# A two-layer decoder trunk on one core: the second mixer's attention is started four dense steps sooner

## The reference

```
q, k, v, qi, ki, wi = split(h @ w_in)          # h: normed x, 512 x 1024
q, k, qi, ki = rope(q), rope(k), rope(qi), rope(ki)
score = sum over 8 heads of relu(qi . ki) * wi # per query block of 128, causal
idx   = top_k(score, 128)
s     = (q . k) / 8, kept only where the key is in idx and causal
out   = softmax(s) @ v
x     = x + norm(out @ w_out)
```

## Time and profile before

| | us |
|---|---|
| median of 3 runs | 1124.03 |
| lowest and highest run | 1121.41, 1128.97 |
| the profiled execution's own time | 1121.3 |
| its span, first to last instruction | 1119.5 |
| TensorE matmul busy | 1077.3 (96%) |
| VectorE busy | 743.7 (66%) |
| ScalarE busy | 542.5 (48%) |
| GpSimd busy | 192.6 (17%) |

### The profile page before, as it was taken

How to read it: one execution, slowest core, us unless ns; L and a number is a source line. 1 busy time by engine, 2 the same in 40 slices (tenths; PEclk the granted TensorE clock), 3 DMA queues, 4 the chain that set the end, 5 groups by cost and what they waited for, 6 DMA issues and landing times. The chain is left out here.

```text
span 1119.5 us, 14906 instructions
## 1 busy us (share of the span) xinstructions
PE 1077.3 (96%) x5433; PEld 865.6 (77%) x5433; DVE 743.7 (66%) x1284; ACT 542.5 (48%) x1014; POOL 192.6 (17%) x338
## 2 busy tenths in 40 slices
PE   7999999999999999999989978999999999999996
PEld 6766678988888888888667755668988888888885
DVE  4354544577688697687478878644587698696684
ACT  6376653445435444435454466653445444444431
POOL 1344530000000000005312368440000000000004
PEclk9999999999999999999999989999999999999998
DMA  7431403824445455422433314003734455355401
GB/s 229 94 77 38 99 16 73 172 62 102 101 106 111 85 113 113 91 61 49 94 76 76 76 39 113 2 1 83 163 71 102 90 113 113 77 112 113 99 15 76
DMA packets 50793, 97.84 MB, mean 87 GB/s; under 512 B 4448, under 2 KB 4640, under 8 KB 50720
## 3 DMA queue, kind: packets, MB, share of 16 engines
q1 hardware_dynamic: 50208, 96.78, 38.7%
q10 hardware_dynamic: 512, 0.11, 0.0%
HBM read 94.78 MB, written 2.10 MB: 87 GB/s over the span
## 5 line engine op out<-in xcount | busy, mean ns | idle before, releaser
L1920 PE MATMUL bank<-r_hi,w_hi 128*128 128x512 f32 (+1 forms) x456 | 177.5, 389 | 0.0
L1921 PE MATMUL bank<-r_hi,w_lo 128*128 128x512 f32 (+1 forms) x456 | 177.4, 389 | 0.0
L1922 PE MATMUL bank<-r_lo,w_hi 128*128 128x512 f32 (+1 forms) x456 | 177.4, 389 | 0.0
L1536 DVE TENSOR_TENSOR w_lo<-w_raw,w_hi 128x1024 fp32r<-128x1024 f32 x84 | 102.1, 1223 | 70.7 <-ACT w_hi L1082 70.6
L1082 ACT ACTIVATE w_hi<-w_raw 128x1024 fp32r<-128x1024 f32 x84 | 87.7, 1055 | 118.8 <-PE bank L1922 82.9
L2261 PE MATMUL bank<-w_hi,hid_hi 128*128 128x512 f32 x336 | 130.7, 389 | 0.0
L2262 PE MATMUL bank<-w_lo,hid_hi 128*128 128x512 f32 x336 | 130.7, 389 | 0.0
L2263 PE MATMUL bank<-w_hi,hid_lo 128*128 128x512 f32 x336 | 130.7, 389 | 0.0
L1091 ACT ACTIVATE w_hi<-w_raw,gT 128x512 fp32r<-128x512 f32 x96 | 64.6, 716 | 107.6 <-DMA w_raw<-in_w_mlp_up 76.1
L776 POOL TENSOR_TENSOR acc<-acc,G 128x512 f32<-128x512 f32 x8 | 13.0, 1653 | 594.3 <-ACT waste L950 594.3
L1930 PE MATMUL bank<-w_hi,r_hi 128*128 128x512 f32 x240 | 101.4, 423 | 5.2 <-DVE w_lo L1313 3.5
(11 more groups left out here) (198 smaller groups left out, 2135.7 us busy)
## 6 DMA issues: line engine op xcount, KB each, us to landing
w_raw<-in_w_mlp_up SPq DMA_DIRECT2D x64, 512.0 KB, 6.5
w_raw<-in_w_mlp_down SPq DMA_DIRECT2D x64, 512.0 KB, 6.9
w_raw<-in_b_w_in SPq DMA_DIRECT2D x16, 512.0 KB, 6.5
w_raw<-in_a_w_in SPq DMA_DIRECT2D x8, 512.0 KB, 6.5
w_raw<-in_a_w_out SPq DMA_DIRECT2D x8, 512.0 KB, 5.9
w_raw<-in_b_w_out SPq DMA_DIRECT2D x8, 512.0 KB, 6.2
X<-in_x SPq DMA_DIRECT2D x4, 512.0 KB, 6.6
w_raw<-in_a_w_in SPq DMA_DIRECT2D x8, 256.0 KB, 7.3
```

The source lines that it names most:

```text
L1536: nc.vector.tensor_tensor(half_of(w_lo[:, u % 2, :], a), b_of(PRODUCTS[i][1], a), half_of(w_hi[:, u % 2, :], a).bitcast(f32), ALU.subtract ...
L1920: nc.tensor.matmul(bank, whi, xhi, start=start, stop=False)
L1921: nc.tensor.matmul(bank, wlo, xhi, start=False, stop=False)
L1922: return nc.tensor.matmul(bank, whi, xlo, start=False, stop=stop)
```

## The change

Four dense steps of the input projection (16 to 19) move from ahead of the loop into it, so the loop starts after step 15, and with them two query tiles (14, 15). The fill table has 18 steps in place of 14: steps 16 to 23, then output steps 0 to 9 as before but in later iterations. The order of pairs takes both query blocks 0 and 1 of one head half first. The high and low halves of output weights 60 to 63 come in later iterations, as do the transposes of updated X blocks 0 and 1. Block 2 has had 3 top-k rounds when the loop starts, where it had 7, and the schedule of rounds in the loop is new.

```diff
-         ((0, 0), (1, 0), (0, 1), (1, 1), (0, 2), (1, 2), (0, 3), (1, 3)))
+         ((0, 0), (0, 1), (1, 0), (1, 1), (0, 2), (1, 2), (0, 3), (1, 3)))
...
-FILL_IN = (12, 20)
+FILL_IN = (12, 16)
...
-        {0: (0,), 1: (1,), 3: (2,), 4: (3,), 5: (4,), 6: (5,), 7: (6,), 8: (7,), 10: (8,), 11: (9,), 12: (10,), 13: (11,),
-         14: (12,), 15: (13,)})
+        {-1: (0, 1), 0: (2,), 1: (3,), 2: (4,), 3: (5,), 5: (6,), 6: (7,), 8: (8,), 9: (9,), 10: (10, 11), 11: (12,), 12: (13,), 13: (14,), 14: (15, 16), 15: (17,)})
...
-          {-1: ((2, 0),), 0: ((2, 1),), 4: ((2, 2),), 5: ((2, 3),)})
-H_TURN = ({13: (0,), 15: (1,)}, {10: (0,), 15: (1,)})
-
-SPLITS = ({-1: (4,), 1: (5,), 6: (6,), 8: (7,), 9: (8,), 10: (9,)}, {1: (60,), 4: (61,), 5: (62,), 6: (63,)})
+          {-1: ((1, 2),), 0: ((1, 3),), 2: ((2, 0),), 3: ((2, 1),), 7: ((2, 2),), 8: ((2, 3),)})
+H_TURN = ({13: (0,), 15: (1,)}, {13: (0,), 16: (1,)})
+
+SPLITS = ({-1: (4,), 1: (5,), 6: (6,), 8: (7,), 9: (8,), 10: (9,)}, {4: (60,), 6: (61,), 7: (62,), 8: (63,)})
...
-FILL_OUT = (12, 4)
+FILL_OUT = (12, 8)
...
-                    for qn in range(12, 18):
+                    for qn in range(12, 16):
...
             split(59)
-            q_high(1, 14)
-            q_high(1, 15)
-            q_scaled(1, 2, 0)
-            q_scaled(1, 2, 1)
...
             split(59)
-            q_low(1, 14)
-            top_rounds(2, 5)
-            q_low(1, 15)
-            top_rounds(2, 7)
-
-
-            ROUNDS_2 = (8, 9, 10, 12, 13, 14, TOPK // 8)
-            ROUNDS_3 = (0, 1, 2, 3, 4, 5, 6, 8, 10, 12, 14, TOPK // 8)
+
+
+            ROUNDS_2 = (5, 7, 9, 11, 13, 14, TOPK // 8)
+            ROUNDS_3 = (0, 1, 2, 3, 4, 6, 8, 10, 12, 14, 15, TOPK // 8)
...
-            for s in range(8, 20):
+            for s in range(8, 16):
                 in_work(1, s)
...
                 if s in (12, 13):
                     queries_turned(1, s)
-                if s in (16, 17):
-                    queries_turned(1, s - 2)
```

More of the change, by code:

```diff
@@ L195, in t_order @@
         order += [("q", 8), ("q", 9), ("ki_tok",), ("q", 10), ("ki_back",), ("q", 11), ("k", 4), ("k", 5), ("k", 6)]
-        order += [("k", 7), ("q", 12), ("q", 13), ("q", 14), ("q", 15)]
+        order += [("k", 7), ("q", 12), ("q", 13)]
     for n in range(-1, 17):
```

## The result

The changed kernel takes a median of 1128.51 us (20 runs, 1126.20 to 1129.67), the kernel before 1122.12 us beside it (20 runs, 1120.63 to 1128.97). The ratio is 1.0047, interval 1.0037 to 1.0057: by it some 5.3 us slower. That is clear of no change, but less than the 1% that I called telling. The profiled execution's own time is 1126.2 us, where the one before had 1121.3.

A forecast was written before the change was run, and what follows sets the result against it. VectorE was taken to bound the stage up to turn 8's mask, 2.8 us sooner; TensorE's road behind it goes from 87.4 to 94.1, ending the stage 3.8 later: 1121.3 + 3.8 = 1125.1, given as 1126, range 1116 to 1132.

The forecast's parts named there:

- Turn 8 masked: End of turn 8's masked scores, the first turn with three key blocks: at 685.5 us, 2.8 us sooner than before.
- VectorE's waits: Avoidable waits in VectorE's chain up to turn 8's mask: 1.31 + 1.73 + 0.5 + 1.53 = 5.1 us taken out.
- The term of 3.0 us for two more rounds: Block 3 has 11 rounds, not 9, by turn 8's masked scores: 2 x 1.52 = 3.0 us more for VectorE.
- From turn 9's first scores to the end: TensorE's road behind turn 8's mask to the stage's end: 94.1 us, where it was 87.4.
- the wait of query 19's transposes: Behind turn 8's mask, a bank copy waits for ScalarE's high half of an output weight: 1.2 us, between 0 and 1.9.
- the waits of 1.39 and 1.24: Two TensorE waits behind turn 8's mask in the kernel before, said to be lost because three more steps cover them.
- the X block in iteration 16: The second X block's transposes have no step beside them: between 0 and 1.9 us, taken as 0.5.
- The gaps: TensorE's gaps from 626 to 685 add up to more than before, the longest put down to VectorE.
- The steps filling the waits: First rival: four moved steps of 2.84 us fill TensorE's idle time and come out whole, 1110 us; chance 7%.
- Half of them: Second rival: VectorE's small waits are more than taken out, turn 8 masked at 680, about 1119 us; chance 25%.
- GpSimd late: Third rival: unit 63's low half ends after TensorE wants it at 704.8, +4 to +7, so 1129 to 1132; chance 13%.
- (c): Pair order in the loop: turns of one and two key blocks change places, changing nothing in the sum to turn 8's mask.

The follow-up runs named there:

- the thinned steps: Changed kernel with nine of twelve matmuls left out of three dense steps ahead of turn 8's mask (ratio to before 1.0044), or three output steps behind it (1.0009).
- the rounds left out: Changed kernel without the first eight top-k rounds of block 3; ratio to the kernel before 0.9964.
- the reverse edit: Kernel before with the changed kernel's schedule of block 3's rounds, two more ahead of turn 8's last masked scores; ratio to the kernel before 1.0000.
- the two edits: Changed kernel with block 3's old schedule of rounds and output weights' high halves behind the next iteration's first copies; ratio to the kernel before 0.9998.
- The one-step version: Kernel before with only dense step 19 and query tile 14 moved into the loop; ratio to the kernel before 0.9982, median 1120.17 us beside 1122.82.
- (rounds): Changed kernel with the kernel before's schedule of block 3's rounds; ratio to the kernel before 1.0032.
- (high halves): Changed kernel with ScalarE's high halves of output weights behind the next iteration's first copies in layer 1; ratio to the kernel before 1.0028.

## Why the prediction was right

**The bound.** That the changed kernel's stage is VectorE's up to turn 8's mask and in the main TensorE's after it is shown from both sides: by the thinned steps and by the rounds left out.

**Turn 8 masked** was said for 685.5 and came at 684.8; the first scores for "about 626" and came at 626.09. VectorE's waits, which I took out of its chain, are out: ahead of the last masked scores of turn 8 only the reciprocals' 0.9 us waits and small ones are left. From the common start to the mask its busy time rose by 1.8 us (51.71 to 53.52), just the 3.0 for rounds less the 1.2 for what falls later; its idle time fell by 5.3 (13.38 to 8.05), where I had 5.1 less 0.5. That 0.7 is the difference. It comes with one of my own signs of being wrong, reciprocal waits under 0.7 us: three are some 0.3, where the shortest wait of a reciprocal in the same part of the kernel before was 0.69. Two of them:

```profile
633.87 0.18 DVE L1395 RECIPROCAL small<-small 128x4 f32<-128x4 f32 x1 [0.30 <-ACT probs L997]
...
654.07 0.18 DVE L1395 RECIPROCAL small<-small 128x4 f32<-128x4 f32 x1 [0.30 <-ACT probs L997]
```

So the chain was a little less stiff than I counted. The term of 3.0 us for two more rounds is confirmed at 2.9. The forecast had to count both, the slack taken away and the rounds put in: the reverse edit shows that the rounds cost nothing while the slack is there.

**From turn 9's first scores to the end** I said 94.1 us and it was 781.01 - 685.04 = 95.97. The terms that were mis-sized:
- the wait of query 19's transposes behind unit 62's high half: 1.2 said, 2.19 measured. My range was 0 to 1.9, the length of the high half, too narrow: the copy behind it takes 1.05 more;
- the waits of 1.39 and 1.24, said to vanish behind three more steps: they came back as 1.02 and 0.66, because unit 63's high half now stands in that iteration, ahead of the copy. I had written that a high half ahead of a copy matters and had looked only at units 60 to 62;
- the X block in iteration 16: 0.5 added. Its waits are 0.34 and 0.39 us, but the kernel before had 0.42 and 0.25 in its last iterations too, and these were in my 87.4 already. So the term was 0.1, not 0.5.

These add 1.0 + 1.7 - 0.4 = 2.3 us; the stretch is 1.9 longer than said. The windows from the mask on show the rest: TensorE's idle time rose by 1.2 us (3.6 to 4.8), where my terms come to 0.9 less, and its busy time by 7.35 (84.01 to 91.36), where 8.5 + 0.4 + 0.4 - 1.7 makes 7.6. So the steps and the half clock (0.98 before, 1.00 after) were sized right to 0.3 us, and the waits were not: I had looked at ScalarE's high halves ahead of the mask and not behind it.

**The stage** was to end 3.8 us later and ended 5.1 later (5.0 from the common start); the added 1.2 or so is the balance of the two steps above, 0.7 sooner and 1.9 later. That they partly cancel is luck. The time that I gave was 2.5 us under the median. Of these 1.1 are the sum's (1125.1 said for the profiled execution, 1126.2 measured); the rest is that the median lies 2.3 above the profiled execution, for which I had allowed 0.9. So the mechanism and the sign were right, and the size was some 1.2 us short of 5.

**The gaps** were to grow, the longest ahead of the second half of turn 8's scores. They did, from 8.8 to 14.9 us ahead of the mask, with VectorE 88% busy (46.57 of the 53.00 us from 632 to 685). But the longest, 3.34, is ahead of a query's transposes and put down to ScalarE's copy: unit 61's high half (676.92, 1.90 us) stands in front of it. I had said that TensorE waits for VectorE there anyway, and in time it made little difference: with the high halves moved behind the copies the mask came 0.4 us sooner. The 2.57 and 2.10 are VectorE's, as said. Half clock beside them I took as 0, with 0 to 3 for its range: the clock in the first stretch is 0.92 in both kernels, and VectorE's chain came on time, so it cost nothing.

**The rivals.** The steps filling the waits (1110 us) did not happen. The Trainium skill (Perfetto Trace Analysis, Optimization Strategy) says that interleaving regimes may help where the most-contended engine changes; here the regimes were already interleaved, and the 6.1 us of TensorE's work that could be taken out of the first one for nothing show that VectorE, not the amount of TensorE's work, set its length. Half of them needed the mask at 680; it came at 684.8. GpSimd late did not happen either, though by my own count its margin was 1.4 us. Unit 63's low half ended at 703.9 (703.4 said):

```profile
698.88 5.01 POOL L788 TENSOR_TENSOR r_lo<-w_raw,r_hi 128x512 fp32r<-128x512 f32 x4
```

TensorE's first step with that unit began at 710.47, not at the 704.8 that I had worked out, since the step at 704.44 was still unit 62's. The margin was 6.6 us and the rival had deserved less than 13%.

**What was not tried.** The order of pairs alone (c), and the later place of the X blocks alone. That the two edits together bring the kernel back to the kernel before says that with the four steps they come to about zero (0.9989 to 1.0006), but not what each costs by itself.

## What to carry to other kernels

Before moving matrix work into an engine's gaps, find out who makes the gaps. If it is another engine that bounds the stretch, filling the gaps gains nothing by itself, and the steps that this pushes behind that engine's last release come out nearly at full length. Count per iteration what stands behind the release before and after. The one-step version pushed nothing there, gave a step to an iteration that had none, and was the only one to gain (0.2%) of those that leave no work out. See also where in the engine's order the gap lies: a step behind the wait does not fill it. When an order changes, look again at what each in-order engine has in front of the copies that others wait for; 1.9 us activations in front of 1.05 us copies were half of this loss (2.6 of 5.0 us).

## What the runs showed of the hardware

- **A closed gap is partly paid back in clock.** Twice TensorE's idle time shrank by more than the stage: 4.2 us against 1.3 (rounds), and behind the mask 3.9 against 2.2 (high halves), with the clock there at 0.97 and 0.98 for 1.00. With both edits the idle time fell by 6.5 us and the stage by 5.8, at 0.99. In the stretch that VectorE bounds the clock fell to 0.74 with thinned steps where it was 0.87, with no time lost. So in these runs the idle time removed was an upper bound of what came back.
- **Executions differ by some 2 to 4 us ahead of the stage, in a step.** Unit 59's low half starts at 622.8 to 623.6 us in seven of the 13 profiled executions and at 625.2 to 626.5 in the other six, and nothing in between. The times of the one-step version part likewise, 1117.1 to 1118.8 and 1121.5 to 1123.5 us. The cause is not known. A difference of 5 us between two profiled executions has to be read from a common mark.
